# First stage of a fused two-block kernel: the first two projection units by column halves between the turned tiles, their weights split ahead, three turned banks instead of five

## The reference, cut to what matters here

```python
h = layer_norm(x, ln_in_g, ln_in_b)             # x: 1024 tokens x 1024
proj = jnp.matmul(h, w_in)                      # here the first 18 tiles of 128 columns
...
mod = jnp.einsum('bd,dn->bn', jax.nn.silu(c), w_ada[layer]) + b_ada[layer]
```

## Time and profile before

| | us |
|---|---|
| median of 3 runs | 3093.25 (3092.14 to 3096.54) |
| the profiled execution, its own time | 3093.8 |
| its span in the profile | 3092.1 |
| TensorE busy over the span | 2859.6 (92%) |
| VectorE / ScalarE / GpSimd busy | 2087.6 / 1577.4 / 479.8 |
| mean granted TensorE clock | 0.962 of full speed |
| first stage (to the barrier behind it) | 0 to 246.6 |
| its first matmul of a unit | 36.79 |
| unit 2, the first of the loop | 64.10 |

### The profile page before, as it was taken

How to read it: one execution, slowest core, us unless ns; L and a number is a source line. 1 busy time by engine, 2 the same in 40 slices (tenths; PEclk the granted TensorE clock), 3 DMA queues, 4 the chain that set the end, 5 groups by cost and what they waited for, 6 DMA issues and landing times. The chain is left out here.

```text
span 3092.1 us, 38488 instructions
## 1 busy us (share of the span) xinstructions
PE 2859.6 (92%) x14048; PEld 2285.6 (74%) x14048; DVE 2087.6 (68%) x2209; ACT 1577.4 (51%) x1950; POOL 479.8 (16%) x486
## 2 busy tenths in 40 slices
PE   7998999999989999999997899999989489999994
PEld 5883566888868678888885788877778368888883
DVE  6998454333338688888885843327765679999995
ACT  4111565432221377787774631125663168778873
POOL 0005400000000021111112312019442000000001
PEclk9999999999999999999998999999999689999997
DMA  7112422652237567986116511100005679999996
GB/s 271 47 34 82 124 75 86 187 177 96 103 127 241 201 235 292 418 364 242 61 55 210 185 46 49 48 7 28 1 18 195 231 278 409 402 406 398 399 382 227
DMA packets 144714, 575.14 MB, mean 186 GB/s; under 512 B 18537, under 2 KB 41857, under 8 KB 104641
## 3 DMA queue, kind: packets, MB, share of 16 engines
q1 hardware_dynamic: 116560, 485.99, 41.6%
q0 software_dynamic: 15840, 57.68, 5.8%
q10 hardware_dynamic: 12176, 29.63, 2.7%
HBM read 584.92 MB, written 82.69 MB: 216 GB/s over the span
## 5 line engine op out<-in xcount | busy, mean ns | idle before, releaser
L2010 DVE TENSOR_TENSOR upper_split<-arena,upper_split 128x2048 fp32r<-128x2048 f32 x185 | 413.1, 2285 | 66.7 <-ACT upper_split L1956 65.6
L3401 DVE TENSOR_TENSOR upper_split_experts<-arena,upper_split_experts 128x1024 fp32r<-128x1024 f32 x288 | 337.5, 1221 | 33.9 <-ACT upper_split_experts L3352 33.7
L1956 ACT ACTIVATE upper_split<-arena 128x2048 fp32r<-128x2048 f32 x184 | 339.4, 1917 | 8.4 <-PE banks L177 6.2
L3352 ACT ACTIVATE upper_split_experts<-arena 128x1024 fp32r<-128x1024 f32 x288 | 288.5, 1053 | 84.1 <-PE banks L177 84.1
L175 PE MATMUL banks<-upper_split_experts 128*128 128x512 f32 x768 | 303.5, 395 | 6.2 <-DVE upper_split_experts L3401 3.6
L175 PE MATMUL banks<-upper_split 128*128 128x512 f32 x744 | 295.8, 398 | 7.3 <-PEq L1603 4.0
L177 PE MATMUL banks<-upper_split_experts 128*128 128x512 f32 x768 | 300.6, 391 | 0.0
L176 PE MATMUL banks<-upper_split_experts 128*128 128x512 f32 x768 | 300.4, 391 | 0.0
L177 PE MATMUL banks<-upper_split 128*128 128x512 f32 x744 | 290.9, 391 | 0.0
L176 PE MATMUL banks<-upper_split 128*128 128x512 f32 x744 | 290.5, 390 | 0.0
L175 PEld LDWEIGHTS banks<-upper_split_experts 128*128 128x128 f32 x768 | 145.3, 189 | 36.2 <-issue 4.2
(11 more groups left out here) (477 smaller groups left out, 6277.3 us busy)
## 6 DMA issues: line engine op xcount, KB each, us to landing
arena<-in_exp_up_k SPq DMA_DIRECT2D x124, 1024.0 KB
arena<-in_gate_up SPq DMA_DIRECT2D x96, 1024.0 KB, 9.2
arena<-in_exp_down_k SPq DMA_DIRECT2D x62, 1024.0 KB
arena<-in_down SPq DMA_DIRECT2D x48, 1024.0 KB, 7.7
upper_middle<-in_gate_up SPq DMA_DIRECT2D x32, 1024.0 KB, 8.8
upper_middle<-in_down SPq DMA_DIRECT2D x16, 1024.0 KB, 7.8
y<-arena POOLq DMA_DIRECT2D x31, 512.0 KB, 2.9
arena<-in_merge_w SPq DMA_DIRECT2D x8, 1536.0 KB, 10.7
```

Of the source, the lines that this page charges most:

```text
L1956: a.activation(rounded(high[s]), raw[s], ACT.Copy).then_inc(high_made[up], 1)
L2010: v.tensor_tensor(rounded(low[s]), raw[s], plain(high[s]), ALU.subtract).then_inc(low_made[up], 1)
L3352: a.activation(rounded(high[n % RING][:, half]), raw[n % RAW][:, half], ACT.Copy).then_inc(high_made, 1)
L3401: v.tensor_tensor(rounded(low[n % RING][:, half]), raw[n % RAW][:, half], plain(high[n % RING][:, half]), ALU.subtract).then_inc(low_made, 1)
```

## The change

The ring of turned banks is three long (banks 4 to 6). Units 0 and 1 work on the first token half right behind each turn of that half, both units for each k; in the second half only unit 0 does, and unit 1's second half follows in one piece. Steps 0 and 1 of the modulation stand between the last products of unit 0, steps 2 to 5 behind unit 0 and ahead of unit 1's second half, steps 6 and 7 behind unit 1. ScalarE and VectorE split the weights of units 0 and 1 before the first turn, and VectorE's statistics of row tiles 5 to 7 stand between its first `low` steps.

```diff
-    TURN = (2, 3, 4, 5, 6)
+    TURN = (4, 5, 6)
+    AHEAD = len(TURN)
...
         @block.tensor
+            def turn(b, k):
+                n = ND * b + k
+                if k == 0:
+                    pe.wait_ge(xhat_done, HT * (b + 1))
+                if n >= AHEAD:
+                    pe.wait_ge(h_high, n - AHEAD + 1)
+                for i in range(HT):
+                    t = pe.transpose(ps[:, TURN[n % AHEAD], i * P:(i + 1) * P],
+                                     x[:, HT * b + i, k * P:(k + 1) * P], core.col("ident"))
+                t.then_inc(turned, 1)
+
             pe.wait_ge(core.loaded, 16)
-            for b in range(2):
-                pe.wait_ge(xhat_done, HT * (b + 1))
-                for k in range(ND):
...
-            for j in range(2):
-                pe.wait_ge(low_made[j], 1)
-                for k in range(ND):
-                    pe.wait_ge(h_low, ND + k + 1)
-                    for c in range(2):
-                        t = product(j, k, c)
-                t.then_inc(done, 1)
-                for k in range(3, 6) if j == 0 else range(6, ND):
-                    modulation(k)
+            for k in range(AHEAD):
+                turn(0, k)
+            for k in range(ND):
+                pe.wait_ge(h_low, k + 1)
+                for j in range(2):
+                    pe.wait_ge(low_made[j], 1)
+                    product(j, k, 0)
+                if k + AHEAD < ND:
+                    turn(0, k + AHEAD)
+            for k in range(AHEAD):
+                turn(1, k)
+            for k in range(ND):
+                pe.wait_ge(h_low, ND + k + 1)
+                t = product(0, k, 1)
+                if k + AHEAD < ND:
+                    turn(1, k + AHEAD)
+                elif k < ND - 1:
+                    pe.wait_ge(act_ready, 2)
+                    modulation(k + AHEAD - ND)
+            t.then_inc(done, 1)
+            for k in range(AHEAD - 1, 6):
+                modulation(k)
+            for k in range(ND):
+                t = product(1, k, 1)
+            t.then_inc(done, 1)
+            for k in range(6, ND):
+                modulation(k)
             pe.wait_ge(ada_used, ND)
...
         @block.scalar
+            for j in range(2):
+                split(0, j)
             for b in range(2):
                 a.wait_ge(xhat_done, HT * (b + 1))
                 for i in range(HT * b, HT * (b + 1)):
                     a.dma_start(m["xhat"][i], x[:, i, :]).then_inc(stored, 16)
                 for k in range(ND):
                     turn(ND * b + k)
-                split(0, b)
...
         @block.vector
-            for b in range(2):
-                if b:
-                    statistics(range(HT + 1, NT))
+            def normalise(b):
                 v.wait_ge(stats, HT * (b + 1))
                 v.wait_ge(rstd_done, b + 1)
...
-            for n in range(ND):
+
+            normalise(0)
+            for j in range(2):
+                split(0, j)
+            for i in range(HT + 1, NT):
+                statistics([i])
+                low(i - HT - 1)
+            low(NT - HT - 1)
+            normalise(1)
+            for n in range(NT - HT, 2 * ND):
                 low(n)
-            split(0, 0)
-            for n in range(ND, 2 * ND):
-                low(n)
-            split(0, 1)
```

More of the change, by code:

```diff
@@ L375, in modulation @@
                 t.then_inc(ada_used, 1)
-            pe.wait_ge(core.loaded, 16)
-            for b in range(2):
-                pe.wait_ge(xhat_done, HT * (b + 1))
-                for k in range(ND):
[L381 to L390, removed]
@@ L417, in turn @@
                 scaled = dict(bias=core.col("ln_in_b", k, k + 1), scale=core.col("ln_in_g", k, k + 1))
-                a.activation(hT[:, k, here], ps[:, TURN[n % 5], :], ACT.Identity, **scaled)
-                a.activation(rounded(hh[:, k, here]), ps[:, TURN[n % 5], :], ACT.Identity, **scaled).then_inc(h_high, 1)
+                a.activation(hT[:, k, here], ps[:, TURN[n % AHEAD], :], ACT.Identity, **scaled)
+                a.activation(rounded(hh[:, k, here]), ps[:, TURN[n % AHEAD], :], ACT.Identity, **scaled).then_inc(h_high, 1)
             def split(i, j):
```

## The result

The changed kernel takes 3102.34 us (median of 7 runs, 3098.97 to 3105.72) against 3092.21 (7 runs, 3087.90 to 3096.54): a ratio of 1.0026, interval 1.0017 to 1.0036, or 5 to 11 us slower, small but clear of the spread of the runs. The forecast was slower by 6.8.

A forecast was written before the change was run, and what follows sets the result against it. The first stage ends a fixed distance behind TensorE's unit loop, paced before 36.79 by ScalarE. Late loads (5.4) with a falling clock (up to 7.4), put at 6.8, make 3093.8 into 3100.6, a median of 3100.0; range 3096.5 to 3103.5.

The forecast's parts named there:

- One for one: End of first stage: a shift of unit 2's first matmul, at 64.10, moves the barrier at 246.66 equally.
- The first half: First token half: first eviction 20.4, not 19.16; turn 8 done at 38.1, not 30.7; last low part follows at 49.8.
- my third rival: Clock low in the first half too: turn 8 at 40, adding 1.9, so +8.7 or more, 3102; chance 0.08.
- one such stretch is absorbed: First half: one low-clock stretch of 3.4 us costs nothing, since VectorE holds TensorE until 31.4 anyway.
- The ring of three: Turned banks, three instead of five: costs nothing, as the next turn is always made inside ScalarE's 1.33 us.
- The late loads: Modulation loads 3 to 5 issued some 16 us later; steps 3 to 5 wait; unit 2 at 69.5, 5.4 later.
- behind them by its bytes: Load 5 behind loads 3 and 4: 1.05 MB at about 400 GB/s is 2.6 us, landing at 60.1.
- The clock: TensorE's granted clock halves in the waits: step 5 costs 0.9 more, products 1.7; unit 2 at 71.5, 7.4 later.
- a clock that falls only behind step 5: Milder case of the half clock on TensorE, falling after step 5: unit 2 about 6.2 us later.
- Loads hidden: Rival at step 3 to 5's buffers: load 5 lands by 55, nothing waits; -1.3, median 3092; chance 0.07.
- Clock full: Rival: loads late but granted clock 1.00 from 48 to unit 2; +4.8 to +5.4, 3098.3; chance 0.32.
- this case: Forecast's main case, late loads plus a fallen clock: put at 6.8 slower, own range +6.0 to +8.5; chance 0.50.

The follow-up runs named there:

- run 5: Changed kernel with the weights of units 2 and 3 loaded on SyncE ahead of modulation load 3; ratio to the kernel before 1.0023 (1.0011 to 1.0035).
- run 1: Changed kernel with modulation steps 0 to 2 early, behind the third turn of the second half; ratio to the kernel before 0.9993 (0.9984 to 1.0001).
- run 2: Kernel before with only modulation steps 0 to 2 moved late, behind unit 0; ratio to the kernel before 1.0037 (1.0024 to 1.0050).
- run 3: Changed kernel with 30 unread matmuls filling TensorE's waits ahead of steps 3, 4 and 5; ratio to the kernel before 1.0034 (1.0023 to 1.0046).
- run 4: Changed kernel with unit 1's second half straight behind step 2, ahead of steps 3 to 7; ratio to the kernel before 1.0030 (1.0018 to 1.0041).
- run 7: Changed kernel with early steps 0 to 2, earlier weights of units 2 and 3, earlier rotary arguments; 3093.25 us against 3094.74, ratio 0.9995.

## Why the prediction was right, point by point

**One for one.** Right: unit 2 and the barrier moved by 9.85 each, and the two agreed to 0.06 us in all seven experiments.

**The first half.** Nearly right. First eviction 20.25 (forecast 20.4), first product 22.63 (22.7), normalising from 28.40 (27.8), turn 8's eviction 38.72 (38.2), last low part's end 50.24 (49.8). The 0.5 fits my third rival, on a small scale: the six products from 22.63 ran at half pace, so turn 3 came at 25.36, its eviction at 26.31 after an idle 1.94, and the low part ahead of the second normalising waited 1.22. I had said that one such stretch is absorbed by VectorE; it isn't quite, since VectorE waits for turn 3 just there. How long this half pace lasts differs between executions (run 5), so that it cost only 0.5 here is in part luck. The ring of three cost nothing that can be seen: run 1 keeps it and loses nothing.

**The late loads.** The mechanism is shown from both sides (run 1 takes it away, run 2 makes it alone), and it is the term that I mis-sized. I had load 3 landing 5.2 us behind its issue, load 5 at 60.1 and full-clock unit 2 at 69.5. Load 3 took 5.4, load 4 landed at 59.8, 4.8 behind it and not 3.3, load 5 at 62.9: issued 0.6 late, then 2.2 more on three loads. From step 5 on, without the wait for load 7 (which the later products hid), my sum ran to 68.9; 2.8 for load 5 and 1.9 for the clock make it 73.6, against 73.95. The step of the forecast that failed is the landing of load 4 3.3 behind load 3 and of load 5 "behind them by its bytes", 2.6 more at 400 GB/s: they landed 4.8 and 3.0 apart, and in 56 to 58, at a mean share of 1.00, the DMA engines moved 287 GB/s. For load 3 the Trainium skill ("DMA: Bandwidth & Descriptors", "Anatomy of one DMA") has a fixed cost of about 2.0 us; that section gives it for DMAs that GpSimd issues, and these are SyncE's. With 2.6 for the bytes it would have had load 3 land in 4.6, an estimate; the trace has 5.4, and the measurement decides.

**The clock.** It fell, as forecast, and cost 1.9 us: 0.85 in step 5 and about 1.0 in the products (6.7 us from 64.72 to 71.43 against 5.7 in run 3, from 63.27 to 68.94; step 4's longer run is hidden by the wait for load 5). I had 0.9 and 1.7. (By these terms a clock that falls only behind step 5 gives 66.5 + 1.7 + 2.4 = 70.6, or 6.5 later, where I wrote 6.2.) The mean of 0.68 in 56 to 58 puts the fall at 56.7, some 0.6 us behind step 3's end, with no wait before it longer than 1.76. The rule of the Trainium skill ("TensorE: Matmul & The Clock Gate", "HAM oscillation"), by which it takes a longer wait than these for the clock to fall, doesn't hold here. Run 3 shows that work in the waits holds it.

**The rivals.** "Loads hidden" is out: three waits of 6.7 us together. "Clock full" is out by the windows, and its size was too small as well: late loads at full clock, as in run 3, put unit 2 at 71.46, past its 69.5.

**The total.** The medians moved by 10.1 and the ratio says 8.0 (5 to 11), against 6.8. The range held it, towards its upper end, since the loads were slower than I let them be. That it did is in part luck: in the profile the stage's 9.85 lies beyond the +6.0 to +8.5 that I gave this case, and unit 2 at 73.95 beyond my 69.5 to 72.

## What to carry to other kernels

When a step is moved, look at what its end releases, above all a load whose buffer ring is full: here three steps of 1 us, moved by 16 us, cost 10.6 us at unit 2 (run 1 against the changed kernel), where the rest of the change gains 0.7 at most in that profile. An instruction that waits on a DMA in an in-order stream should stand behind all work that doesn't need it, but that alone is no cure while the loads themselves stay chained to late steps. And follow each engine through a moved piece, not only the one that paces the stage.

## What the runs showed of the hardware that I had not expected

The column of the granted clock reads 1.00 in the first 26 us though TensorE isn't at full pace there: 12 transposes take 2.79 us at 17.20 and 1.47 at 38.08, and the first products at 22.63 last 0.80 instead of 0.50. That the clock was at half there, and the column lacks it, is borne out by runs 1, 3 and 4, which are the same up to there. Their first product lasts 0.50, those from 25.5 on 0.78, and the column does show it; this is run 1:

```profile
24.00:26.00 2.00, 2.00 (x8) 1.66 (x7) 1.97 (x5) 0.35 (x2) 0.00 (x0) 0.50 1.02 408
```

So where durations and column differ this early in a span, I go by the durations. Why the column lacks it, no run tells.

With a mean busy share of 1.00 or a little above, the DMA engines moved 287 GB/s in the changed kernel's window of 56 to 58 and 407 in that of 60 to 62:

```profile
60.00:62.00 2.00, 1.72 (x8) 0.00 (x0) 0.00 (x0) 0.00 (x0) 0.00 (x0) 0.50 1.06 407
```

A share near 1 did not tell here how soon the next load lands. From the issue of load 3 to the landing of load 5 it took 10.9 us in runs 1 and 7 (issues 0.86 us apart, the `trig` store moved only behind them), 11.8 in run 2 (0.86 apart, with the store), and 12.2 to 13.2 in the changed kernel and runs 3, 4 and 5 (1.9 apart, with the store). Run 1's loads start on an empty queue as well, so the start alone isn't the difference. The store's small packets are a part: in run 7 it goes by itself, and it takes 0.70 of all engines' time in one microsecond and moves 0.2 MB in it:

```profile
52.00:53.00 1.00, 1.00 (x10) 0.21 (x12) 0.00 (x0) 1.00 (x1) 0.00 (x0) 1.00 0.70 205
```

What makes the rest, the distance of the issues, uneven engines or the spread between executions, no run here tells.
